# Loading both halves of x ahead of the first weight chunk, using that chunk in halves, and moving the parameter loads to GpSimd's queue

## The reference

```python
def mlstm_mixer(x, w_in, gate_b, conv_w, norm_g, w_out):
    ...
    proj = x @ w_in                                   # 1024 x 3080
    qk = jax.nn.silu(causal_dwconv(proj[..., :nqk], conv_w))   # nqk = 1024
    v = proj[..., nqk:nqk + nv]
    o = proj[..., nqk + nv:nqk + nv + D_MODEL]
    gates = proj[..., nqk + nv + D_MODEL:] + gate_b   # 8 columns
    i_pre = gates[..., :H]
    log_f = jax.nn.log_sigmoid(gates[..., H:])
    ...                                               # chunked scan, norm, @ w_out
```

## Time and profile before

| | |
|---|---|
| median of 3 runs | 1002.29 us (1001.18 to 1004.8) |
| profiled execution, its time | 1004.83 us |
| profiled execution, its span in the trace | 1003.0 us |
| PE busy in the span | 976.8 us (97%) |
| DVE busy | 650.4 us (65%) |
| ACT busy | 492.7 us (49%) |
| POOL busy | 56.8 us (6%) |
| read from HBM | 198.00 MB, 198 GB/s over the span |

### The profile page before, as it was taken

The page is one execution under the profiler, slowest core; times in us unless marked ns, Lnnn a source line. Parts: engine busy times, 40 slices in busy tenths (PEclk is TensorE's granted clock), DMA queues, the critical chain, the costliest instruction groups (busy, mean ns, idle before and its releaser), DMA issues.

```text
span 1003.0 us, 14917 instructions
## 1 busy us (share of the span) xinstructions
PE 976.8 (97%) x6233; PEld 884.1 (88%) x6233; DVE 650.4 (65%) x748; ACT 492.7 (49%) x657; POOL 56.8 (6%) x94
## 2 busy tenths in 40 slices
PE   6999999999999999999999999999999999999996
PEld 6888988989999999898899999997987799999996
DVE  4885467659777665875787776448767685445453
ACT  4657353545645455254375445437565473343431
POOL 1000131001000002100100000002100100000000
PEclk9999999999999999999999999999999999999998
DMA  8864445726988876192398888553554236565511
GB/s 268 292 210 148 146 152 187 250 86 208 343 291 275 288 267 230 49 332 88 118 351 290 287 285 289 197 166 93 201 177 126 84 138 219 178 200 171 196 56 42
DMA packets 114528, 200.03 MB, mean 199 GB/s; under 512 B 5123, under 2 KB 85369, under 8 KB 111389
## 3 DMA queue, kind: packets, MB, share of 16 engines
q1 hardware_dynamic: 111340, 188.38, 55.6%
q0 software_dynamic: 2832, 10.16, 3.0%
q10 hardware_dynamic: 288, 0.52, 0.1%
HBM read 198.00 MB, written 1.05 MB: 198 GB/s over the span
## 4 chain that ended last, share of the span: by engine, by line
PE 87%; DVE 5%; ACT 2%; SPq 1%; issue 1%; DMA 1%; POOL 1%; DVEq 0%; POOLq 0%; ACTq 0%
PE WB L337 12%; PE WB L333 12%; PE WB L330 12%; PE YB L354 10%; PE YB L358 10%; PE YB L349 10%; PE YB L394 6%; PE WB L349 2%; PE WB L358 2%; PE WB L354 2%; PE WB L436 1%; PE WB L656 1%; PE WB L637 1%; ACT wh L1023 1%; DMA raw<-in_mlstm_w_in 1%
## 5 line engine op out<-in xcount | busy, mean ns | idle before, releaser
L1565 DVE TENSOR_TENSOR wl<-raw,wh 128x2048 fp32r<-128x2048 f32 (+1 forms) x151 | 345.6, 2296 | 192.0 <-ACT wh L1023 191.4
L1023 ACT CAST wh<-raw 128x2048 fp32r<-128x2048 f32 (+1 forms) x151 | 286.6, 1902 | 44.2 <-PE YB L358 24.3
L330 PE MATMUL WB<-XH,wh 128*128 128x256 f32 x1024 | 145.9, 285 | 0.0
L333 PE MATMUL WB<-XH,wl 128*128 128x256 f32 x1024 | 144.1, 284 | 0.0
L337 PE MATMUL WB<-XL,wh 128*128 128x256 f32 x1024 | 143.7, 283 | 0.0
L330 PEld LDWEIGHTS WB<-XH,wh 128*128 128x128 f32 x1024 | 135.0, 192 | 3.5 <-DVE SM L2001 0.3
L333 PEld LDWEIGHTS WB<-XH,wl 128*128 128x128 f32 x1024 | 132.6, 193 | 0.0
L337 PEld LDWEIGHTS WB<-XL,wh 128*128 128x128 f32 x1024 | 132.1, 192 | 0.0
L349 PE MATMUL YB<-wh,FHT 128*128 128x512 f32 x360 | 111.9, 392 | 0.0
L354 PE MATMUL YB<-wl,FHT 128*128 128x512 f32 x360 | 111.1, 390 | 0.0
L358 PE MATMUL YB<-wh,FLT 128*128 128x512 f32 x360 | 111.0, 389 | 0.0
(11 more groups left out here) (308 smaller groups left out, 1116.9 us busy)
## 6 DMA issues: line engine op xcount, KB each, us to landing
raw<-in_mlp_w SPq DMA_DIRECT2D x64, 1024.0 KB, 6.2
raw<-in_w_ada SPq DMA_DIRECT2D x24, 1024.0 KB, 5.1
raw<-in_mlstm_w_in SPq DMA_DIRECT2D x12, 1024.0 KB, 7.7
raw<-in_w_ffn_gate SPq DMA_DIRECT2D x11, 1024.0 KB, 5.4
raw<-in_w_ffn_up SPq DMA_DIRECT2D x11, 1024.0 KB, 5.3
raw<-in_w_ffn_down SPq DMA_DIRECT2D x11, 1024.0 KB, 4.9
raw<-in_mem_w_kv SPq DMA_DIRECT2D x8, 1024.0 KB, 5.2
raw<-in_xattn_wq SPq DMA_DIRECT2D x8, 1024.0 KB, 7.1
```

The costliest lines, as they stand in the source:

```text
L330: e.matmul(o, H[:, at(k)], xh[:, k, :], start=k == 0, stop=False)
L333: e.matmul(o, L[:, at(k)], xh[:, k, :], start=False, stop=False)
L1023: f = e.copy(w[:, 0:a * b], raw[:, 0:a * b])
L1565: f = e.tensor_tensor(L[:, 0:a * b], raw[:, 0:a * b], H[:, 0:a * b].bitcast(F32), ALU.subtract)
```

## The change

x's second half is issued by SP directly behind its first, and the load of chunk 0 is cut into two loads of 512 KB, the first on a semaphore of its own (`d_half`). The gate weights, the eleven parameter rows, and the two gate biases are issued by GpSimd instead of SP. DVE now makes the high part and the low part of chunk 0's first half; ACT makes the high part of the second, DVE its low part. PE works on ("in", 0) in a new function `first()`, with two banks and in halves of the features. On ACT the casts of the later chunks (`hi_to`) stand at other places.

```diff
 # tensor
-            def x_hi(k):
-                if k % 4 == 0:
-                    e.wait_ge(*act_front["x", 1, k // 4])
-            def x_lo(k): ...
+            def first():
+                Ws = [bank(("in", 0, f))[:, 0:256] for f in range(2)]
+                def part(w, x, kh, start=False, stop=False):
+                    for f in range(2):
+                        for k in range(4 * kh, 4 * kh + 4):
+                            p = e.matmul(Ws[f], w[0][:, 256 * k + 128 * f:256 * k + 128 * f + 128], x[:, k, :],
+                                         start=start and k == 0, stop=stop and k == 7)
+                    return p
+                for kh in range(2):
+                    e.wait_ge(*act_front["x", 1, kh])
+                    e.wait_ge(*(w_half["hi"] if kh == 0 else w_hi[0]))
+                    part(WH, XH, kh, start=True)
+                    e.wait_ge(*(w_half["lo"] if kh == 0 else w_lo[0]))
+                    part(WL, XH, kh)
+                for kh in range(2):
+                    e.wait_ge(*dve_front["x", 1, kh])
+                    p = part(WH, XL, kh, stop=True)
+                return p
 # scalar
             for t in range(2):
                 for q in range(2):
                     blocks(("x", t, q), q, t, 4, act_front, pe_turn["x", t, q])
-                if t == 0:
-                    hi_to(0)
+            at[0] = 1
+            e.wait_ge(*landed(0))
+            e.copy(WH[0][:, 1024:2048], RAW[0][:, 1024:2048]).then_inc(w_hi.add(0))
+            hi_to(M["in", 1])
+            e.wait_ge(d_gates, 48)
+            e.wait_ge(*dve_zero["gates"])
+            e.copy(GH[:, :, 0:4], GRAW[:, :, 0:4])
+            e.copy(GH[:, :, 32:36], GRAW[:, :, 4:8]).then_inc(act_front.add("gates"))
+            hi_to(M["in", 2])
             for j in range(4):
-                hi_to(M["in", j] + 3)
-                W = bank_of.get(("in", j), WB[0])
                 e.wait_ge(*pe_front["in", j])
-                e.copy(QP[:, 2 * j:2 * j + 2, 3:259], halves(W[:, :])).then_inc(act_front.add(("qp", j)))
...
+                else:
+                    W = bank_of.get(("in", j), WB[0])
+                    e.copy(QP[:, 2 * j:2 * j + 2, 3:259], halves(W[:, :])).then_inc(act_front.add(("qp", j)))
+                    freed["in", j] = act_front["qp", j]
+                hi_to(M["in", j] + 3)
 # vector
+            e.wait_ge(d_half, 16)
+            e.tensor_copy(WH[0][:, 0:1024], RAW[0][:, 0:1024]).then_inc(w_half.add("hi"))
+            e.wait_ge(*w_half["hi"])
+            e.tensor_tensor(WL[0][:, 0:1024], RAW[0][:, 0:1024], WH[0][:, 0:1024].bitcast(F32), ALU.subtract
+                            ).then_inc(w_half.add("lo"))
+            x_low(0, 0)
+            x_low(1, 0)
+            at[:] = [1, 1]
+            e.wait_ge(*w_hi[0])
+            e.tensor_tensor(WL[0][:, 1024:2048], RAW[0][:, 1024:2048], WH[0][:, 1024:2048].bitcast(F32), ALU.subtract
+                            ).then_inc(w_lo.add(0))
+            x_low(0, 1)
+            x_low(1, 1)
 # sync: both halves of X, then chunk 0 in two loads, then chunks 1, 2, ...
-                load(t)
-            e.dma_start(GRAW, w_in[:, 3072:3080].rearrange("(k p) c -> p k c", p=128)).then_inc(d_gates, 16)
+            for kh, done in enumerate((d_half, s_raw[0])):
+                dst = RAW[0][:, 1024 * kh:1024 * kh + 1024].rearrange("p (a b) -> p a b", a=4)
+                e.dma_start(dst, chunks[0][1][:, 4 * kh:4 * kh + 4, :]).then_inc(done, 16)
```

More of the change, by code:

```diff
@@ L285, in build_program @@
         ends, freed, bank_of, bv_of = {}, {}, {}, {}
-        d_idn, d_rows, d_gates, d_tab, d_mem, d_mod, d_wm, d_tb, d_lam, d_out0, d_out1 = (
-            sem("in_" + n) for n in "idn rows gates tab mem mod wm tb lam out0 out1".split())
+        d_idn, d_half, d_rows, d_gates, d_tab, d_mem, d_mod, d_wm, d_tb, d_lam, d_out0, d_out1 = (
+            sem("in_" + n) for n in "idn half rows gates tab mem mod wm tb lam out0 out1".split())
         d_x = [sem(f"in_x{t}") for t in range(2)]
         d_bv = [sem(f"in_bv{n}") for n in range(2)]
-        w_hi, w_lo, w_ada, w_pool = (count(n) for n in "w_hi w_lo w_ada w_pool".split())
+        w_hi, w_lo, w_half, w_ada, w_pool = (count(n) for n in "w_hi w_lo w_half w_ada w_pool".split())
         pe_turn, pe_front, pe_mlstm, pe_rows, pe_xa, pe_mlp, pe_pool, pe_mod, pe_mix, pe_ffn = (
@@ L445, in tensor @@
                     turn(("x", t, q), lambda k: X[:, t, 128 * k:128 * k + 128], range(4 * q, 4 * q + 4), pe_turn)
-            def x_hi(k):
-                if k % 4 == 0:
-                    e.wait_ge(*act_front["x", 1, k // 4])
-            def x_lo(k):
-                if k % 4 == 0:
-                    e.wait_ge(*dve_front["x", 1, k // 4])
-            for j in range(4):
[L456 to L459, removed]
+            def first():
[16 more added lines that the diff above has]
+                return p
+            for j in range(4):
+                m = M["in", j]
+                if j == 0:
+                    p = first()
+                else:
+                    W = bank(("in", j))
+                    for f in range(2):
+                        p = fm(m, 8, 256, 128 * f, W[:, 256 * f:256 * f + 256])
                 p.then_inc(pe_front.add(("in", j)))
@@ L1039, in scalar @@
                     blocks(("x", t, q), q, t, 4, act_front, pe_turn["x", t, q])
[L1040 to L1041 removed]
+            at[0] = 1
[7 more added lines that the diff above has]
+            hi_to(M["in", 2])
             for j in range(4):
[L1043 to L1044 removed]
                 e.wait_ge(*pe_front["in", j])
[L1046 to L1047 removed]
                 if j == 0:
+                    for f in range(2):
+                        p = e.copy(QP[:, f, 3:259], bank_of.get(("in", 0, f), WB[0])[:, 0:256])
+                    p.then_inc(act_front.add(("qp", 0)))
+                    for f in range(2):
+                        freed["in", 0, f] = act_front["qp", 0]
                     W = bank_of.get("cols", WB[0])
@@ L1574, in vector, with x_low @@
             e.memset(GT[0:64, :], 0.0).then_inc(dve_zero.add("gt"))
[L1575 to L1585, removed]
+            def x_low(t, q):
+                W = bank_of.get(("x", t, q), WB[0])
+                tk = slice(128 * t, 128 * t + 128)
+                e.wait_ge(*act_front["x", t, q])
+                e.tensor_tensor(XL[:, 4 * q:4 * q + 4, tk], W[:, :].rearrange("p (k c) -> p k c", k=4),
+                                XH[:, 4 * q:4 * q + 4, tk].bitcast(F32), ALU.subtract
+                                ).then_inc(dve_front.add(("x", t, q)))
+                freed["x", t, q] = dve_front["x", t, q]
+            e.wait_ge(d_half, 16)
[11 more added lines that the diff above has]
+            x_low(1, 1)
             def conv(j):
@@ L2330, in sync @@
                 e.dma_start(X[:, t, :], I["x"][0, 128 * t:128 * t + 128, :]).then_inc(d_x[t], 16)
-                load(t)
-            e.dma_start(GRAW, w_in[:, 3072:3080].rearrange("(k p) c -> p k c", p=128)).then_inc(d_gates, 16)
[L2333 to L2344, removed]
+            for kh, done in enumerate((d_half, s_raw[0])):
+                dst = RAW[0][:, 1024 * kh:1024 * kh + 1024].rearrange("p (a b) -> p a b", a=4)
+                e.dma_start(dst, chunks[0][1][:, 4 * kh:4 * kh + 4, :]).then_inc(done, 16)
+            for n in range(1, len(chunks)):
                 if n == N["dv", 1]:
```

23 lines of the change are left out of this document (18 added, 5 removed).

## The result

The changed kernel takes 1006.96 us (median of 5 runs, 1006.5 to 1007.23), the kernel before 1003.01 us (median of 5, 1001.18 to 1004.8): ratio 1.004, 95% interval 1.0025 to 1.0054. It is slower, by 3.95 us in the medians, which is under the 0.5% that was set as the bound of "no change". The forecast was +4.1 us.

What follows compares the result with a forecast made beforehand. PE, busy 976.8 of 1003.0 us, was taken as the bound. ("in", 0) at 14.4 and chunk 5's subtraction at 39.65, plus 17.2, put the panel at 56.9, not 52.77: +4.1, 1006.4 us, range 1001.5 to 1009.5.

Steps and rivals of the forecast that it cites:

- The second bank decides the start: At ("in", 0): PE waits for x's second low part to free a bank and begins at 14.4, not 11.98.
- The slow stretch of the first chunk: In ("in", 0): 4.6 us at 1.2 GHz after idling, so the chunk takes 7.85 us and ends at 22.25.
- Gate columns: Between ("in", 1) and ("in", 2): PE no longer waits, which wins 1.7 us back; ("in", 2) ends at 36.9.
- The cast of chunk 5 behind the copy: ACT's cast follows the copy of ("in", 2); DVE's subtraction starts at 39.65, panel ("vo", 1) at 56.9 after PE idles 2.9 us.
- The sum: Panel ("vo", 1) begins at 56.9 instead of 52.77, so the whole kernel loses 4.1 us.
- The fall of the clock behind the second wait: Rival: the clock falls again in the second idle of 2.9 us, costing 2.1 us, 1008.5; chance 0.08.
- from there on no wait of PE depends on what the change edits: Behind the start of panel ("vo", 1) at 52.77, so its shift is what the whole kernel gains or loses.
- nothing makes it good: Behind panel ("vo", 1): ACT, DVE and PE all stay late by about the same +4.1 us.
- The late half: Rival at chunk 0's load: GpSimd's small pieces delay the half, each us adds one, 1008.8 at 11.5; chance 0.2.
- Only one wait bites: Rival at the two added waits: 1003.9 without the later one, 1000.2 without the bank wait; together chance 0.1.
- faster: Rival: neither added wait bites and PE keeps all it can win, 5.0 us, 997.3; chance 0.05.
- It costs nothing that GpSimd issues the parameters: At the parameter rows: GpSimd's loads are there ahead of 19, first user at 22, 3 us of cover.

Runs made afterwards that it cites:

- changed twice: The changed kernel, measured a second time without any edit: 1006.96 us first, 1007.5 us again.
- banks free early: Changed kernel with the low parts of x's first token half made ahead of all work on chunk 0: 1001.66 us.
- first wait filled: Changed kernel with 40 unused turns of a 128x128 block put between the turns of x and the first chunk: 1005.39 us.
- parameters on SyncE: Changed kernel with the parameters issued by SyncE again, behind chunk 1, GpSimd left with its tables: 1006.15 us.
- both repairs: Changed kernel with x's first low parts ahead of chunk 0 and ScalarE's casts of chunks 3 to 6 ahead of the copies: 998.61 us, again 998.63.
- the filled waits: Changed kernel with unused TensorE work ahead of the first chunk (1005.39 us) or, separately, ahead of the panel ("vo", 1)'s second bank (1005.54 us).

## Why the prediction was right

*The second bank decides the start.* Shown. Forecast 14.4, measured 13.88. By terms: half at 8.90 for 9.1, cast 0.69 for 0.75, subtraction 1.23 start to end but 1.14 from start to start for 1.2, hand-overs nearly nothing for 0.2. Moving the two low parts alone took the wait for the banks away.

*The slow stretch of the first chunk.* Right: 7.75 us for 7.85, though so close by luck: in the other four profiles with this wait left empty it is 7.10, 7.42, 7.76 and 8.15. It was a reading of matmul spacing, since the granted clock of before says 1.00 where the matmuls run at half pace; in the changed kernel the granted clock agrees with the spacing, 0.50 from 13.88 to 18.00. The filled wait showed the cause.

*Gate columns.* Right: no wait, ("in", 2) from 30.43 to 36.19 in place of the 31.1 to 36.9 of the forecast.

*The cast of chunk 5 behind the copy.* Shown, by the edit that puts it back. Forecast 39.65 for VectorE's subtraction, measured 38.81; the 17.2 us behind it held to a hundredth. Wait 2.74 for 2.9, panel at 56.02 for 56.9.

*The sum is right in part by luck.* Three terms behind it were off, and they cancel. The panel's start was forecast 0.9 late (+4.1 for +3.25), of which 0.5 is the start of the first chunk. The fall of the clock behind the second wait, which I had put among the rivals at 0.08 and 2.1 us, did come, at 1.6 us, in both profiles of the changed kernel. Of the five profiles with this wait left open (changed twice, banks free early, first wait filled, parameters on SyncE) four show it, all but the last, so it deserved far more than 8 in 100. And "from there on no wait of PE depends on what the change edits" and "nothing makes it good" did not hold: 1.9 us come back near 690 us in every profile with the new start. By the landmark the change costs 4.8, near 723 us it costs 3.3, at the end of the two profiled executions 1.7. The median has 3.95, with an interval from 2.5 to 5.4 us; the profiled execution of the kernel before is 1.8 us above its median, that of the changed one 0.5 below its own. So the two added waits and their places were foreseen and are shown; that +4.1 meets 3.95 so closely is not to their credit.

*The late half.* The landing was near, 8.90 for 9.1, by two errors that cancel: the lower bound of 8.73 was too high, as the half is cast at 8.28 without the small pieces, and these cost 0.6 us and not 0.4. They did not cost the several us of the rival. *Only one wait bites* and *faster* are out: both waits are in both profiles of the changed kernel, and each costs by itself. *It costs nothing that GpSimd issues the parameters* was right for the changed kernel and too short: the parameter rows did not hold TensorE up, but the move has a worth of its own, 1.3 us on the kernel before, and 9 us (998.6 to 1007.7) once the banks are free early and the casts go ahead of the copies.

## What to carry to other kernels

A function that takes two buffers up front waits for the later one: look up which operation frees it, and where that operation now stands in its engine's program. When work is made available earlier, the operations that free things (copies out of PSUM, low parts) must not slide behind work that waits for loads; nor must a cast slide behind the copy of a result that comes late. And a part that is neutral in one version can be what another version stands on, so a bundle of three edits should be taken apart before it is dropped: here one part won a little, two lost, and with two small reorderings the whole is 5.3 to 5.8 us faster than before. And an edit at the start can move a wait 600 us later: compare the whole of two profiles, and not only the part that was edited.

## What the runs showed of the hardware

The clock falls in some executions behind an idle time of 2.74 us and not in others, though TensorE's program around it is the same: slow matmuls at once (56.02, landmark 68.54), after 1 us (52.17 with the banks free early), or none at all (54.75 with the parameters on SyncE). One such fall is worth 1.6 us; runs of one kernel scatter by 0.7 to 5.7. Near 690 us the same goes with the program and not with chance: slow matmuls behind 1.96 and 1.99 us of waiting in the two profiles with the old start, full pace behind 1.61 to 1.65 us in the eleven with the new one. The kernel with both repairs, which has neither wait, spreads by only 1.4 and 2.2 us in its two measurements, but with 6 runs each against mostly 12 of the others, and the first five runs of the changed kernel, with both waits, spread by only 0.7; that it spreads less for lack of waits was not shown. The Trainium skill (TensorE: Matmul & The Clock Gate, Part 1) says that an idle engine falls to 1.2 GHz and is given 2.4 again once busy; the filled waits agree, with a granted clock of 1.00 behind the second where the empty one has 0.53.
